# An expert loop on one Trainium2 core: the low halves of the weights in three wide VectorE operations in place of six

## The reference, cut to what matters

```python
def expert_block(args):
    xblk, e = args                                   # 128 rows, one expert
    g, u = jnp.split(xblk @ w_expert_gu[e], 2, axis=-1)      # (1024, 512)
    return (jax.nn.silu(g) * u) @ w_expert_down[e]           # (256, 1024)

yb = lax.map(expert_block, (xb, block_e)).reshape(n_rows, d)
routed = jax.ops.segment_sum(yb * row_w[:, None].astype(yb.dtype), row_tok, num_segments=n_tok)
```

## Time and profile before

| | |
|---|---|
| median of 3 runs | 1804.72 us (1803.86 to 1805.12) |
| profiled execution, its own time | 1809.02 us |
| its span, first to last instruction | 1807.2 us |
| mean granted TensorE clock | 0.990 |
| TensorE busy | 1714.1 us (95%) |
| VectorE busy | 1144.4 us (63%) |
| ScalarE busy | 795.4 us (44%) |
| DMA moved | 357.79 MB, 198 GB/s on average |

### The profile page before, as it was taken

The page is one execution under the profiler, slowest core; times in us unless marked ns, Lnnn a source line. Parts: engine busy times, 40 slices in busy tenths (PEclk is TensorE's granted clock), DMA queues, the critical chain, the costliest instruction groups (busy, mean ns, idle before and its releaser), DMA issues.

```text
span 1807.2 us, 32703 instructions
## 1 busy us (share of the span) xinstructions
PE 1714.1 (95%) x7475; PEld 1239.4 (69%) x7476; DVE 1144.4 (63%) x1695; ACT 795.4 (44%) x1094; POOL 536.1 (30%) x569
## 2 busy tenths in 40 slices
PE   6999999998889999899999999999999999999987
PEld 1545454446754487788887777888888877888864
DVE  4773775403877869567538788553767677265646
ACT  0211112122231032466547788563766677265624
POOL 2000000004732310244334444443444344344321
PEclk9999999999999999999999999999999999999999
DMA  9652000011344331769859899866889689587863
GB/s 380 256 229 95 1 0 0 1 37 42 116 154 156 120 148 65 287 201 327 267 96 374 291 330 344 283 185 189 267 274 346 198 287 372 100 287 230 233 211 139
DMA packets 95504, 357.79 MB, mean 198 GB/s; under 512 B 19390, under 2 KB 19551, under 8 KB 86758
## 3 DMA queue, kind: packets, MB, share of 16 engines
q1 hardware_dynamic: 65298, 288.49, 41.7%
q0 software_dynamic: 30160, 68.76, 17.0%
q10 hardware_dynamic: 4, 0.02, 0.0%
HBM read 330.96 MB, written 70.62 MB: 222 GB/s over the span
## 4 chain that ended last, share of the span: by engine, by line
PE 71%; DMA 11%; DVE 7%; issue 4%; ACT 3%; DVEq 2%; SPq 1%; POOL 1%; ACTq 1%; POOLq 0%
PE psum L1333 8%; PE psum L1335 7%; PE psum L1334 7%; DMA sum_rows<-arena,idxs 7%; PE psum L1059 7%; PE psum L1164 5%; PE psum L1068 4%; PE psum L1320 4%; PE psum L1357 3%; PE psum L1355 3%; PE psum L1356 3%; PE psum L1006 3%; PE psum L1099 3%; DMA raw_weights<-in_w_gu 3%; ACT split_weights L681 1%
## 5 line engine op out<-in xcount | busy, mean ns | idle before, releaser
L1913 DVE TENSOR_TENSOR split_weights<-raw_weights,split_weights (+1 forms) x366 | 428.3, 1220 | 33.1 <-ACT split_weights L681 26.8
L681 ACT ACTIVATE split_weights<-raw_weights (+1 forms) x366 | 363.9, 1061 | 19.7 <-SPq L507 12.5
L1333 PE MATMUL psum<-split_weights,split_rows 128*128 (+1 forms) x832 | 336.3, 404 | 2.3 <-DVE split_rows L1902 2.3
L1335 PE MATMUL psum<-split_weights,split_rows 128*128 (+1 forms) x832 | 326.4, 392 | 0.0
L1334 PE MATMUL psum<-split_weights,split_rows 128*128 (+1 forms) x832 | 325.2, 391 | 0.0
L681 ACT ACTIVATE arena<-psum 128x1024 f32<-128x1024 f32 (+6 forms) x187 | 154.5, 831 | 378.5 <-PE psum L1059 107.1
L645 POOL DMA_INDIRECT sum_rows<-arena,idxs x102 | 175.2, 1718 | 227.4 <-DMA sum_rows<-arena,idxs 179.6
L681 ACT ACTIVATE split_rows<-psum 128x256 fp32r<-128x256 f32 (+1 forms) x209 | 148.0, 708 | 158.9 <-PE psum L1341 151.0
L631 POOL COPY idxg<-idxT 128x1 uint32 (+1 forms) x107 | 85.9, 803 | 365.3 <-DVE split_rows L1902 293.1
L1335 PEld LDWEIGHTS psum<-split_weights,split_rows 128*128 128x128 f32 x832 | 157.0, 189 | 35.1
L1333 PEld LDWEIGHTS psum<-split_weights,split_rows 128*128 128x128 f32 x832 | 157.8, 190 | 31.7 <-DVE split_rows L1902 2.5
(11 more groups left out here) (299 smaller groups left out, 2304.4 us busy)
## 6 DMA issues: line engine op xcount, KB each, us to landing
raw_weights<-in_w_gu SPq DMA_DIRECT2D x62, 2048.0 KB
raw_weights<-in_w_dn SPq DMA_DIRECT2D x62, 1024.0 KB
arena<-in_w_ada SPq DMA_DIRECT2D x12, 2048.0 KB, 8.7
arena<-in_toks SPq DMA_DIRECT2D x18, 512.0 KB, 9.5
arena<-job_rows SPq DMA_DIRECT2D x16, 512.0 KB, 3.7
arena<-in_w_vog SPq DMA_DIRECT2D x1, 4160.0 KB, 14.0
arena<-in_w_qk SPq DMA_DIRECT2D x1, 4096.0 KB, 17.0
arena<-in_w_out SPq DMA_DIRECT2D x2, 2048.0 KB, 9.5
```

The lines of the kernel that those rows point to most:

```text
L681: return act.activation(o, i, ACT.Copy)
L1333: mm(bank(3 + p), xk, part(par, 0, 512 * k), start=(k == 0), stop=False)
L1335: ins = mm(bank(3 + p), xl, part(par, 0, 512 * k), start=False, stop=(k == 7))
L1913: tt(cols(wsplit, (1 - par) * (2 * WE) + (WE + 1024 * c), 1024), cols(raw, (1 - par) * WE + 1024 * c, 1024), high, ALU.subtract).then_inc( ...
```

## The change

`w_low` walks over its chunks in pairs. For each pair it waits until both high halves are made, subtracts 2,048 columns in one operation, and raises `lo_split` by two. It is called in the same places with the same ranges (0 to 3, 4 and 5, 0 and 1, 2 and 3). ScalarE's high halves stay at 1,024 columns each, and no other engine's program is touched.

```diff
+            def wide(t, o):
+                return cols(t, o, 2048)
+
             def w_low(e, par, chunks):
 
-                for c in chunks:
-                    dve.wait_ge(S("hi_split"), 6 * e + (c + 1))
-                    high = cols(wsplit, (1 - par) * (2 * WE) + 1024 * c, 1024).bitcast(F32)
-                    tt(cols(wsplit, (1 - par) * (2 * WE) + (WE + 1024 * c), 1024), cols(raw, (1 - par) * WE + 1024 * c, 1024), high,
-                       ALU.subtract).then_inc(S("lo_split"), 1)
+                for c in chunks[::2]:
+                    dve.wait_ge(S("hi_split"), 6 * e + (c + 2))
+                    high = wide(wsplit, (1 - par) * (2 * WE) + 1024 * c).bitcast(F32)
+                    tt(wide(wsplit, (1 - par) * (2 * WE) + (WE + 1024 * c)), wide(raw, (1 - par) * WE + 1024 * c), high,
+                       ALU.subtract).then_inc(S("lo_split"), 2)
```

## The result

The changed kernel takes 1844.38 us (median of 4 runs, 1841.57 to 1847.38) against 1804.92 us (4 runs) for the kernel before: a ratio of 1.0212, 95% interval 1.0193 to 1.0231. That is 39 us slower. The forecast was 14 us slower, 1818.7 us, with a range up to 1832. The direction was right, the size was not: the measured time lies 12 us above the range.

A forecast was written before the change was run, and what follows sets the result against it. TensorE was taken to bound the kernel. Terms of 16.6 + 6.6 + 6.2 - 0.5 + 1.0 made 29.9 us gross, net +13.6 after give-back, taken as 14 on the median 1804.72: 1818.7 us, range 1809 to 1832.

The forecast's parts named there:

- What bounds the kernel: TensorE, busy for 95% of the span, bounds it; VectorE, busy for 63%, matters only where TensorE waits for it.
- full steps: 43 expert-loop steps with four low-half operations ahead of h_rows; with highs in time they become 10.1 to 10.2 us.
- the wide operation: VectorE's doubled low-half operation: 2.28 us long, saving 0.07 us per pair, 13 us of busy time over 183 pairs.
- The point that decided: Step at 809.02: x_low ends at 813.25, before second high plus 0.63 us (814.18), so the wide operation starts late.
- the rival of fewer, larger operations: Faster, 1799 us, if x_low and not the highs held chunks 4, 5; 1794 by operation count alone; chance 0.06.
- The start of the loop: Ahead of the loop, the first expert's wide chunks 4, 5 delay x_low and TensorE's first gate/up product: +1.0 us.
- What is given back: In DMA-bound runs of full steps, stretched steps let transfers catch up, shrinking waits of 27.5 and 12.5 us; net +13.6 us.
- Waits for sum_rows would shrink: ScalarE's evacuation waits for the scatter-add of rows to DRAM, 27.5 us before, would become smaller.
- The other steps: Loop steps with one pair or none ahead of h_rows: zero cost, slack covers the delay; without cover 6 us.
- gross sum without give-back: Rival: load issues slip with the steps, DMA idles, every term stands, 1834.6 us; chance 0.15 for 1826 or more.

The follow-up runs named there:

- scatter-add first: Kernel after, with GpSimd issuing each block's scatter-add ahead of the gather instead of behind it: 1822.75 us, ratio 1.0087 to the kernel before.
- the narrow one in its own order: Kernel before (operations of 1,024 columns), with GpSimd issuing the scatter-add ahead of the gather: 1804.65 us, ratio 0.9991 to the kernel before.
- the run with the late start alone: Kernel before, its 1,024-column operations kept, but the first of each pair waits for both highs: 1828.03 us, ratio 1.0124 to the kernel before.

## Why the prediction was wrong

- **What bounds the kernel, the full steps, the wide operation: right.** 183 operations of 2.289 us (2.28 forecast), full steps of 10.11 and 10.23 us (10.1 to 10.2), VectorE 14.5 us less busy (13). The point that decided, x_low's end against the second high plus 0.63 us, decided as said, and the rival of fewer, larger operations did not come.
- **The start of the loop: right.** The wait of TensorE's first gate/up product for x_low went from 2.28 us to 3.34: +1.06, with 1.0 forecast. An earlier end of the routing, 1.2 us in this execution, hides it in the span.
- **What is given back: somewhat too large.** Of a gross 30 us I gave back 16. The wide kernel whose scatter-adds are not late (scatter-add first) costs 16 us against the kernel before and 18 against the narrow one in its own order, so 12 to 14 came back: 2 to 4 us less than forecast. In the run with the late start alone the waits for DMA did vanish (27.5 to 1.1 us, 12.5 to 1.8 us), but of the 27.5 us only 11.6 lay in the 43 full steps, by my sum over the timeline. The rest lay in the 60 others, and those took 562.2 us before and 563.8 in that run: there the end of the waits gave nothing that shows.
- **Waits for sum_rows would shrink: the failed step that made the miss.** They rose to 49.0 us. The forecast went through TensorE, ScalarE, VectorE and SyncE and never asked what a VectorE operation of twice the length does to GpSimd. The trace was at hand: before the change the index copy had a free length of 0.18 us and a median of 1.01 us, and each held one ended with a low. That term was put at nothing. It is 22 us by the exchange of GpSimd's order, or 16 to 18 net of what the longer operation saves. With it the sum closes: 14 forecast, 2 to 4 given back too much, 22 for GpSimd, against 39.5 measured.
- **The other steps: zero was wrong for the same reason.** They grew by 8.8 us, for example the step at 798.17, 10.98 us with an evacuation 2.96 us late. With the late start alone they grew by 1.6 us only.
- **The range.** My upper end, 1832, stood just under the gross sum without give-back (1834.6). It had no room for a cost that I had not named.

## What to carry to other kernels

A wide operation that waits for two producers starts one producer later; where its engine has no slack, that is a loss of the producer's whole time against a few hundredths of a microsecond per operation saved. Before lengthening VectorE operations with two SBUF inputs, look at GpSimd's shortest instructions: if some of them end with the VectorE operation that they meet, GpSimd's DMA issues can come later by the added length, and the cost is what waits for them. Give back an expected loss only for waits that lie on the path; count those in steps with slack as nothing.

## What was not expected of the hardware

TensorE's clock fell after some of its stalls. These are windows of the kernel after (busy us of the engines, then granted clock, DMA share, GB/s):

```profile
819.00:831.00 12.00, 9.59 (x46) 7.81 (x46) 8.36 (x7) 8.27 (x10) 5.54 (x4) 1.00 1.03 372
832.00:842.00 10.00, 10.00 (x44) 8.59 (x45) 6.36 (x6) 4.60 (x6) 6.40 (x4) 0.86 0.94 340
```

TensorE had waited 2.85 us for h_rows at 831.82. In the step that follows, the granted clock averages 0.86, so part of it ran at the lower of the two levels (1.2 GHz), and the step took 10.78 us in place of 9.43. The kernel after has four such steps, which take 6.4 us more together from the turn to the last gate and up product; the kernel before has one, 1.7 us. The waits before the four were 2.65 to 3.36 us. But the length of one wait does not decide it: a wait of 2.75 us ahead of the step at 989.83 was followed by no slow stretch, and in the run with the late start alone one of 1.94 us was, at 886.66. So a late scatter-add may cost more than its own wait. No run was made to separate this from the rest.

A GpSimd instruction that copies 128 words was held up to 1.80 us by one VectorE operation; the sizes are above. VectorE starts 0.63 us after its producer ends where the addresses of the operation are computed between the wait and the operation, and 0.64 us in the kernel after. For the fixed addresses ahead of the loop it was 0.03 us before and 0.13 us after. I read the difference as the register instructions, but no run was made without them.
